# Two orders of work (VectorE at the end, ScalarE in attention) and eight unread products on TensorE before the last expert

## The reference

```python
# third head group ("C"): compressed, selected and sliding-window attention of the same queries
p_c = masked_softmax(einsum('bqhd,bnd->bhqn', qi, kc) * scale, ...)      # compressed keys
...
out = gates[..., 0] * o_c + gates[..., 1] * o_s + gates[..., 2] * o_w

# experts: top-1 group, then top-2 experts in it, 16 experts in all
hid = silu(t @ w_gate[e]) * (t @ w_up[e])
y   = y + (hid * combine[:, e, None]) @ w_down[e]

x = x + g2 * y
return rms_norm(x, final_norm)
```

## Time and profile before

| what | value |
| --- | --- |
| median of 3 runs | 772.02 us (770.45 to 775.83) |
| profiled execution, own time | 771.39 us |
| its span (first to last instruction) | 769.6 us |
| PE busy | 682.3 us (89%) |
| DVE busy | 328.8 us (43%) |
| ACT busy | 180.2 us (23%) |
| POOL busy | 116.6 us (15%) |
| transfers | 172.90 MB, mean 225 GB/s |

### The profile page before, as it was taken

The page is one execution under the profiler, slowest core; times in us unless marked ns, Lnnn a source line. Parts: engine busy times, 40 slices in busy tenths (PEclk is TensorE's granted clock), DMA queues, the critical chain, the costliest instruction groups (busy, mean ns, idle before and its releaser), DMA issues.

```text
span 769.6 us, 9939 instructions
## 1 busy us (share of the span) xinstructions
PE 682.3 (89%) x3865; PEld 397.2 (52%) x3869; DVE 328.8 (43%) x782; ACT 180.2 (23%) x435; POOL 116.6 (15%) x164
## 2 busy tenths in 40 slices
PE   1699899999999999887999994899999999999544
PEld 1574346667666598555554554445443444444211
DVE  2203757856467433585723228562111121212355
ACT  3204315122121121455721113111111121111113
POOL 8700122314032057000000000000000000000300
PEclk9999999999999899898999996999999999999977
DMA  9999103793330120850062117998999999999962
GB/s 330 374 258 377 16 1 110 245 311 114 110 110 1 22 35 2 273 187 34 1 219 55 55 37 261 410 327 287 392 403 395 422 397 418 387 413 403 421 261 111
DMA packets 76239, 172.90 MB, mean 225 GB/s; under 512 B 21890, under 2 KB 39004, under 8 KB 72860
## 3 DMA queue, kind: packets, MB, share of 16 engines
q1 hardware_dynamic: 70912, 157.85, 56.6%
q0 software_dynamic: 2608, 9.18, 3.2%
q10 hardware_dynamic: 2668, 5.18, 1.8%
HBM read 156.33 MB, written 15.87 MB: 224 GB/s over the span
## 4 chain that ended last, share of the span: by engine, by line
PE 75%; DVE 11%; POOL 4%; DMA 3%; issue 3%; ACT 3%; POOLq 0%; DVEq 0%; ACTq 0%
PE ps L1050 13%; PE ps L1207 7%; PE ps L2463 7%; PE ps L1083 6%; PE ps L2430 5%; PE ps L1044 5%; PE ps L2541 2%; DMA y<-expert_rows,slot 2%; PE ps L1078 2%; PE ps L2547 2%; PE ps L2427 2%; PE ps L2454 2%; POOL lev L1805 2%; PE ps L2551 2%; PE ps L670 2%
## 5 line engine op out<-in xcount | busy, mean ns | idle before, releaser
L1050 PE MATMUL ps<-gu,xgT 128*128 128x512 f32 x224 | 97.4, 593 | 3.4 <-DVE xgT L1148 2.3
L2463 PE MATMUL ps<-hT,winr 128*128 128x512 f32 x144 | 73.2, 617 | 0.2
L1689 POOL DMA_INDIRECT xg<-xn_rows,list x15 | 13.9, 927 | 381.5 <-PE ps L1019 183.6
L1050 PEld LDWEIGHTS ps<-gu,xgT 128*128 128x128 f32 x224 | 42.0, 190 | 54.1 <-issue 54.1
L1044 PE MATMUL ps<-gu,xgT 128*32 128x256 f32 (+1 forms) x416 | 52.1, 487 | 8.0 <-DMA gu<-in_w_up 8.0
L1207 PE MATMUL ps<-wout,yT 128*128 128x512 f32 x128 | 56.3, 595 | 0.0
L1916 POOL TENSOR_TENSOR cc<-low,lev 128x512 f32<-128x512 f32 x20 | 30.2, 1518 | 131.1 <-DVE low L2250 105.6
L1083 PE MATMUL ps<-dn,hidT 128*128 128x512 f32 x112 | 49.4, 594 | 0.0
L2054 DVE SCALAR_TENSOR_TENSOR acc<-ada,st,acc 128x512 f32<-128x512 f32 x56 | 48.5, 866 | 1.3
L2430 PE MATMUL ps<-hT,wind 128*128 128x512 f32 x96 | 42.3, 594 | 0.0
L1123 ACT ACTIVATE sg<-ps 128x512 f32<-128x512 f32 (+2 forms) x16 | 7.2, 450 | 134.8 <-PE ps L1050 90.5
(11 more groups left out here) (451 smaller groups left out, 1083.9 us busy)
## 6 DMA issues: line engine op xcount, KB each, us to landing
dn<-in_w_down SPq DMA_DIRECT2D x16, 2048.0 KB, 20.6
gu<-in_w_gate SPq DMA_DIRECT2D x14, 2048.0 KB, 13.9
gu<-in_w_up SPq DMA_DIRECT2D x14, 2048.0 KB, 19.2
ada<-in_w_ada SPq DMA_DIRECT2D x12, 2048.0 KB, 12.0
expert_rows<-zero SPq DMA_DIRECT2D x12, 512.0 KB, 6.6
gu<-in_w_gate SPq DMA_DIRECT2D x8, 512.0 KB, 5.0
gu<-in_w_up SPq DMA_DIRECT2D x8, 512.0 KB, 6.5
expert_rows<-yo ACTq DMA_DIRECT2D x7, 512.0 KB, 10.5
```

The lines of the kernel that those rows point to most:

```text
L1050: ins = nc.tensor.matmul(PS[2 * b + w][:, :], T["xgT"][:, k, :], w_in[:, w, k, :], start=(k == 0), stop=(k == KT - 1))
L2463: ins = t.matmul(bank[:, :], w(k), T["hT"][:, k, :], start=(k == 0), stop=(k == KT - 1))
```

## The change

Three edits, and nothing else.

1. ScalarE, attention step 9 (`CMP_TRANSPOSES - 1`): the copies of transposed probabilities come ahead of the exponentials of that step. In all other steps the order stays.
2. TensorE, slot 15: between the down product of slot 14 and the gate and up products of slot 15 stand eight products of 128x512 whose result nothing reads, on data that is there already (`xgT` of slot 15, already waited for).
3. VectorE, the end: `hidm` of slot 15 comes ahead of all additions of `rows_added`. Two of the `y1` additions follow, then `yc` of slot 15, the other two of `y1`, and then for each tile the `y2` addition directly ahead of the addition of `pe_back`'s result.

```diff
-    def act_attention_step(act, s):
+    def act_exps(act, s):
...
+    def act_prob_copies(act, s):
+        a = nc.scalar
         if TR_LAG <= s < NPS + TR_LAG:
...
+    def act_attention_step(act, s):
+
+        if s == CMP_TRANSPOSES - 1:
+            act_prob_copies(act, s)
+            act_exps(act, s)
+        else:
+            act_exps(act, s)
+            act_prob_copies(act, s)
...
             if n == E - 1:
                 pe_down(pe, n - 1)
+                pe.wait_ge(sem("xgT_a"), n + 1)
+                pe.wait_ge(sem("xgT_d"), n + 1)
+                for _ in range(8):
+                    t.matmul(PS[3][:, :], idf[:], T["xgT"][:].rearrange("p a b -> p (a b)")[:, 0:512], start=True,
+                             stop=True)
             pe_gate_up(pe, n, b)
...
             if n == E - 1:
                 dve_output(dve, n - 1)
-                rows_added(0)
-                rows_added(1, (0, 1))
             dve_product(dve, n, n % 2)
-            if n == E - 1:
-                rows_added(1, (2, 3))
...
+        rows_added(0, (0, 1))
         dve_output(dve, E - 1)
+        rows_added(0, (2, 3))
         for i in range(ST):
+            rows_added(1, (i,))
             dve.wait_ge(sem("oproj_mm"), ST + 1 + i + 1)
```

## The result

| | before | after |
|---|---|---|
| median of 20 runs, us | 773.49 (766.13 to 777.91) | 768.82 (762.82 to 775.04) |
| profiled execution, us | 771.39 | 769.11 |
| its span, us | 769.6 | 767.3 |
| its mean granted clock | 0.957 | 0.957 |

The measured ratio, over the executions that ran undisturbed, is 0.9946, 95% interval 0.9928 to 0.9964: 4.2 us faster (2.8 to 5.6); it is not the quotient of the two medians, which lie 4.7 us apart. Forecast were 6.4 us (ratio 0.9917, outside the interval) and 765.6 us; the measured time lies in the forecast range, 3.2 us above the forecast.

The account below looks back on a forecast made before the run. TensorE was taken as nearly full from 390 to 720 us, with gains only in its waits in attention and at the end. 3.7 + 0 + 2.7 = 6.4 us off 772.02 gave 765.6 us, range 762.5 to 769.5.

Parts of the forecast that it names:

- Attention, 3.7 us: Attention steps 9 to 11: earlier ScalarE copies start step 10's transposes 2.0 us earlier; full clock gives another 1.75; together 3.7.
- the case for which the prediction gave 2.0: Attention: against executions of the kernel before that kept full clock at 349, the ScalarE edit is worth 2.0 us.
- Eight products, 0: Slot 15: products keep full clock, gate and up finish 1.8 us earlier, but this ends in a wait, so counted 0.
- The cover that I named: Slot 15: the wait for the last down weights hides the eight products' gain, up to 1.8 us without it.
- The end, 2.7 us: Slot 15's down waits for its weights, runs at low clock; last addition ends at 758.3 instead of 761.02, gaining 2.7 us.
- TensorE is full, so the shift reaches the expert stage: After attention: TensorE, busy 313.59 of 330 us from 390 to 720, carries attention's 3.7 us into the expert stage.
- the prediction's own sign: Expert stage: the forecast is wrong if its start is not 3.7 us earlier.
- Attention gives 2.0 or less, or the low level comes back at another gap: Rival, attention: low level not in every run or back at another gap, so 2.0 us or less; 767.3 us, chance 0.13.
- The weight stream: Rival, expert stage: full weight transfers take back attention's gain, leaving only 2.7 us; 769.3 us, chance 0.08.
- The full clock in the last down product: Rival, slot 15: TensorE keeps full clock into the last down, 1.4 us more gain; 764.2 us, chance 0.17.
- Slower: Rival, end: low clock for all work added or moved there, 5.3 us later; 775.3 us with attention low too, chance 0.03.
- no change: Rival: the passed additions return behind yc and attention's gap is refilled; within 2 us of 772, chance 0.03.

Follow-up runs that it names:

- e2: Kernel before with only the new VectorE order at the end; 770.93 us, ratio 0.9986 to the kernel before.
- e3: Kernel before with only the eight unread products ahead of slot 15's gate and up; 773.79 us, ratio 1.0012 to the kernel before.
- e10: Whole change plus three unread products ahead of the last down, but ScalarE's old order at step 9; 766.86 us, ratio 0.9947 to the kernel before.
- e1: Kernel before with only ScalarE's copies moved ahead of the exponentials at step 9; 767.41 us, ratio 0.9954 to the kernel before.
- e11: Kernel before with ScalarE's edit alone, plus unread products in the output stage's short waits and the routing; 766.86 us, ratio 0.9945 to the kernel before.
- e12: Kernel before, none of the three edits, plus unread products in the output stage's short waits and the routing; 770.70 us, ratio 0.9995 to the kernel before.
- e8: Kernel before, old order kept, with three unread products in TensorE's 3.35 us attention wait; 773.48 us, ratio 1.0021 to the kernel before.
- e4: Whole change without the eight products, so both reorderings only; 768.43 us, ratio 0.9950 to the kernel before.
- e5: Whole change, slot 15's down reading slot 14's weights without waiting for its own, which still load (wrong result); 761.3 us, ratio 0.9871 to the kernel before.
- e6: Whole change plus three unread products between the transpose of hidm and the last down; 766.38 us, ratio 0.9927 to the kernel before.
- e7: Whole change plus fifteen unread products in TensorE's routing waits (7, 2 and 6); 765.30 us, ratio 0.9934 to the kernel before.

## Why the prediction was right, and where it missed

- **Attention, 3.7 us: right.** The forecast start of L636 was 0.14 us behind `cn`; it is 0.06 (345.71 to 345.77). The level stays full and the profiles give 3.68 (10.82 - 7.14), or about 2.9 against the executions of e2, e3 and e10, whose low stretch was shorter (A about 10.0). In the times e1 has 3.6 and e11 against e12 3.8. The Trainium skill ("TensorE: Matmul & The Clock Gate", Part 1) says that the clock gate is free-running and doesn't reset with the kernel; the lengths of A for the old order agree, from 9.96 to 10.82 us. None of the unfilled ones was at full level throughout, so the case for which the prediction gave 2.0 was not seen; e8, at full level by its fillers, has A 8.61, and against it the edit would be worth 1.5 (8.61 - 7.14).
- **Eight products, 0: right, though not where I put them.** No gain was seen in e3 and e4. The products started at 725.41 instead of 722.5 and ended at 732.5, 2.0 us after 730.5, when the weights had come before. The reason is slot 13's down product, which stands still inside itself (last section). Gate and up took 3.66 us (forecast 3.9). The cover that I named, the wait for the last down weights, swallowed the delay: 3.18 us of it were left.
- **The end, 2.7 us: right.** The weights landed 26.5 us behind their issue (forecast 26.6), down ran at the low level in 3.64 us (3.37), the idle ahead of `yc` was 4.64 us (4 to 6), and D is 44.91 where 47.38 - 2.7 = 44.7 was forecast. e5 shows that this wait holds the end, e6 that the level of down is a term of its own (forecast 1.4, D gives 1.25).
- **The sum, 6.4 us: too large by 2.2.** The step that failed is "TensorE is full, so the shift reaches the expert stage". By the prediction's own sign it failed there: the start of the experts was to be 3.7 us earlier, but slot 0's gate and up come 2.8 us earlier and slot 1's 0.12 us later. The earlier trace rows are busy time over 330 us, and full on the mean hides waits of 1.2 to 7 us between 400 and 490. They are no longer than before, but the granted clock may fall in or shortly behind them, and what that costs differs between executions of the same code: up to slot 1, e1, e4, e5, e6 and after run the same instructions, and B is 147.1 in e1, e5 and e6, 150.5 in e4 and 152.4 in after; before, e2 and e3 have 147.1, and e10, the same up to there, 152.4. The changed kernel's profile gave back 5.26 us. For that profile the account closes: 1.46 us earlier at `cn`, A 3.68, B -5.26 and D 2.47 make 2.35, and its span is 2.3 us shorter.
  That the same loss, in some executions, makes the 2.2 us by which the measured gain falls short is likely from the spread above, but not shown; edit 3's small gain in the times (e2) would do for a part of it.
- **The rivals.** "Attention gives 2.0 or less, or the low level comes back at another gap" is the one whose mechanism was seen, in its second half (the low level came back at another gap), and its time of 767.3 is nearer to 768.82 than mine; but the runs of before stood 1.5 us higher than the median that I started from, and by the ratio (4.2 gained) it is 767.8. The weight stream falls by C. The full clock in the last down product did not come: it was low there, and e6 prices it. Slower and no change did not come.

**What stays open.** Among profiles with the output stage unfilled, the level fell between attention and the routing in 1 of 4 where it was low in attention (e10, of before, e2, e3, e10) and in 4 of 7 where attention kept it (after, e4, e7, e8, of these and e1, e5, e6). That could mean that a gain in attention makes later falls more frequent, but so few profiles don't show it. The times speak weakly for a cost of the kind: e1 and e2 sum to 4.6 us where their distances A and D give 3.7 + 2.0 = 5.7, and e8 saved 2.2 us in A and nothing in the times. Nor is it explained why e2's times gave 1.1 us for 2.0 in D.

## What to carry to other kernels

Carry a gain to the end of the span only stage by stage: take the time between two fixed points in each profile, and ask of every TensorE wait over a microsecond whether the granted clock can fall in it. A gain of 3 to 4 us upstream can be lost in such a wait that nobody touched. Here one unread product in each short wait kept the level in two profiles, and together with those of the routing and e6's three at the end they brought the change from 4.2 to 8.6 us. Where a transfer ended the last wait, the work moved ahead of it cost nothing and gained nothing.

## What was unexpected

**Runs of one kernel lie 12 us apart** (766.13 to 777.91 before). Over 29 other runs the kernel before took from 767.66 us at a granted clock of 0.964 to 777.7 at 0.945; time and clock correlate with -0.90 (changed kernel, 20 runs: -0.78, 762.82 at 0.964).

**TensorE stands still inside a product group.** Slot 13's down product is 32 records, 1.93 us at full level, in the kernel before in one piece and in the changed kernel torn:

```profile
717.99 1.93 PE L1078 MATMUL ps<-dn,hidT 128*32 128x256 f32 x32
...
718.55 0.64 PE L1089 MATMUL ps<-dn,hidT 128*32 128x256 f32 x4 [0.38 <-issue]
719.96 1.10 PE L1089 MATMUL ps<-dn,hidT 128*32 128x256 f32 x6 [0.78 <-issue]
721.40 1.52 PE L1089 MATMUL ps<-dn,hidT 128*32 128x256 f32 x22 [0.34 <-issue]
```

From 718.55 to 722.92 are 4.4 us, and the profile names nothing that the gaps wait for. All profiles of e1 to e8 have it, that of before does not, though e8 changes nothing in this stretch nor near it. The transfers are full there (414 to 423 GB/s), and nearly as full at the same place of the kernel before (401 to 421); the cause wasn't tried. It would have cost time where no wait for weights follows it.
